# Experts of a routed MLP: sorted by token count and taken four at a time, in place of fixed pairs in rounds

## What is computed

```python
def expert_mlp(t, w1, w3, w2):
    return (jax.nn.silu(t @ w1) * (t @ w3)) @ w2

def hier_moe(h, w_rg, b_rg, w_re, b_re, w1, w3, w2):
    ...                     # best of 4 groups, then the best 2 of its 8 experts, per token
    cw = jnp.einsum('tk,tkn->tn', wts, jax.nn.one_hot(eid, N_EXPERTS, dtype=F32))
    y = jnp.zeros_like(t)
    for e in range(N_EXPERTS):
        y = y + (cw[:, e:e + 1] * expert_mlp(t, w1[e], w3[e], w2[e])).astype(t.dtype)
    return y.reshape(shp)
```

## Time and profile before

| | |
|---|---|
| Median of three runs | 1081.12 us |
| Lowest of the three | 1079.55 us |
| Profiled execution, its own time | 1078.98 us |
| Its span, first to last instruction | 1077.5 us |
| Mean granted TensorE clock | 0.985 of 2.4 GHz |
| TensorE busy with products | 1024.2 us (95%) |
| VectorE, ScalarE busy | 332.3 us, 365.1 us |
| Moved by DMA | 284.14 MB, 127505 packets |

### The profile page before, as it was taken

One profiled execution on the slowest core, in us unless ns is written; L12 is line 12 of the kernel. 1 busy time (PEld: TensorE's weight loads), 2 busy tenths in 40 slices (PEclk: granted clock), 3 DMA queues, 4 the chain that ended last, 5 costly groups with the idle time before them and its releaser, 6 DMA issues.

```text
span 1077.5 us, 14121 instructions
## 1 busy us (share of the span) xinstructions
PE 1024.2 (95%) x5184; PEld 615.0 (57%) x5184; DVE 332.3 (31%) x803; ACT 365.1 (34%) x659; POOL 65.8 (6%) x110
## 2 busy tenths in 40 slices
PE   4799999999999999999998999999999999999994
PEld 2568686868687877788765444444334444444441
DVE  2345555555545454552223111010110111110013
ACT  6263637373737373720023212222112221222212
POOL 1020202020202020200000000000000000000000
PEclk9899999999999999999997999999999999999997
DMA  9946262627272715237873999999999999999920
GB/s 347 312 111 180 84 186 77 193 70 200 63 205 58 212 51 156 78 117 230 350 305 130 378 418 417 429 422 422 421 418 420 420 420 419 421 430 422 420 98 40
DMA packets 127505, 284.14 MB, mean 264 GB/s; under 512 B 6336, under 2 KB 100736, under 8 KB 115200
## 3 DMA queue, kind: packets, MB, share of 16 engines
q1 hardware_dynamic: 127152, 283.82, 70.7%
q10 hardware_dynamic: 336, 0.10, 0.0%
HBM read 282.86 MB, written 1.05 MB: 263 GB/s over the span
## 4 chain that ended last, share of the span: by engine, by line
PE 89%; DVE 3%; issue 3%; DMA 2%; SPq 1%; ACT 1%; POOL 0%; DVEq 0%; ACTq 0%; POOLq 0%
PE bank L480 35%; PE bank L775 21%; PE bank L783 10%; PE bank L767 6%; PE bank L793 6%; PE bank L710 3%; DMA arena<-in_w_mod 2%; DVE arena L1487 2%; PE bank L505 1%; PE bank L814 1%; SPq L302 1%; PE bank L512 1%; PE bank L584 1%; PE bank L601 1%; PE bank L610 1%
## 5 line engine op out<-in xcount | busy, mean ns | idle before, releaser
L480 PE MATMUL bank<-arena 128*128 128x256 f32 (+3 forms) x1792 | 403.1, 382 | 4.4 <-DVE arena L1156 3.8
L480 PEld LDWEIGHTS bank<-arena 128*128 128x128 f32 x1792 | 298.9, 191 | 95.1 <-issue 65.6
L775 PE MATMUL bank<-arena 128*64 128x512 f32 x1024 | 226.0, 594 | 0.9 <-ACT arena L1039 0.9
L775 PEld LDWEIGHTS bank<-arena 128*64 128x64 f32 x1024 | 72.1, 137 | 149.9 <-issue 149.9
L783 PE MATMUL bank<-arena 128*64 128x512 f32 x512 | 113.4, 595 | 0.0
L1487 DVE TENSOR_TENSOR arena<-arena,bank 128x512 f32<-128x512 f32 x16 | 16.5, 1029 | 253.3 <-PE bank L775 253.3
L1052 ACT ACT_TABLE_LOAD x16 | 20.5, 1283 | 194.1 <-PE bank L775 194.1
L1491 DVE COPY arena<-bank 128x512 f32<-128x512 f32 x32 | 22.1, 691 | 170.5 <-PE bank L783 170.5
L783 PEld LDWEIGHTS bank<-arena 128*64 128x64 f32 x512 | 35.3, 137 | 65.9 <-issue 64.0
L767 PE MATMUL bank<-arena 128*128 128x128 f32 x544 | 65.8, 281 | 0.6 <-DVE arena L1452 0.6
L767 PEld LDWEIGHTS bank<-arena 128*128 128x128 f32 x544 | 64.2, 197 | 0.7 <-DVE arena L1452 0.7
(11 more groups left out here) (275 smaller groups left out, 879.4 us busy)
## 6 DMA issues: line engine op xcount, KB each, us to landing
arena<-in_w SPq DMA_DIRECT2D x96, 2048.0 KB, 12.1
arena<-in_w_in SPq DMA_DIRECT2D x72, 512.0 KB, 7.0
arena<-in_w_mod SPq DMA_DIRECT2D x12, 2048.0 KB, 8.1
arena<-in_w_proj_a SPq DMA_DIRECT2D x8, 512.0 KB, 3.8
arena<-in_w_proj_b SPq DMA_DIRECT2D x8, 512.0 KB, 5.3
arena<-in_w_out SPq DMA_DIRECT2D x2, 2048.0 KB, 9.8
arena<-in_x SPq DMA_DIRECT2D x4, 512.0 KB, 5.4
arena<-in_ctx SPq DMA_DIRECT2D x2, 512.0 KB, 6.7
```

Of the source, the lines that this page charges most:

```text
L480: i = mm(dst, w(k), rhs(k), start=k == 0, stop=k == KT - 1)
L775: i = mm(acc[SLOTS * b:SLOTS * b + SLOTS, :], xg[:, k, SLOTS * b:SLOTS * b + SLOTS], wtile(kind, b, j)[:, k, :], start=k == 0, stop=k == K ...
```

## The change

The rounds and the fixed pairs are replaced by a list. Experts 0 to 3 stay first, as two pairs with 64 slots each, while VectorE sorts the other 28 by their counts. The 24 with fewer tokens follow as six units of four, with `NARROW` = 32 slots each; the four fullest (`TOP`) come last, in pairs with 64 slots, in a loop of `n_pairs` turns that begins with them and goes on with extra items. An extra item is a further visit to an expert that has more tokens than the slots it was given, and it loads that expert's matrices again. With no such expert `n_pairs` is 2. The eight units before the loop are written out, so `UNROLL` and the loop over groups of pairs go.

What is used more than once: columns of `rk` and `ck` are ranks and weights in list order, `ids_i` the expert numbers, which SyncE reads into registers one by one (`chosen`); `LOADS` is the list of the 84 loads before the loop, `PLACE` their slots. The accumulating banks are no longer cleared by a product with zeros (`zb`); the first `combine`, in unit 1, starts them. The constants, slots and semaphore values:

```diff
-PAIRS = NE // 2
+NARROW = 32
+FIXED = 4
+TOP = 4
+
+UNITS = [(e, 2) for e in range(0, FIXED, 2)] + [(c0, 4) for c0 in range(FIXED, NE - TOP, 4)]
+NU = len(UNITS)
+C_ITEM = NE - TOP
+N_EXTRA = 16
+COLS = NE + N_EXTRA + 2
...
+        KINDS = ("w1", "w3", "w2")
+        LOADS = [(u, k, b) for u, (_, n) in enumerate(UNITS) for k in KINDS for b in range(n)]
+        PLACE = {load: i % len(RING) for i, load in enumerate(LOADS)}
+
+        def wslot(kind, b, u):
+
+            if u == NU:
+                return ring[(len(LOADS) + 2 * KINDS.index(kind) + b) % len(RING)]
+            return ring[PLACE[u, kind, b]]
+
+        def wtile(kind, b, u):
+
+            return wslot(kind, b, u).rearrange("p (k n) -> p k n", n=D if kind == "w2" else F)
+
+        def arrived(u):
+
+            return 16 * sum(UNITS[v][1] for v in range(u % 2, u + 1, 2))
```

SyncE's loads:

```diff
-            for j in range(UNROLL):
-                load_pair(j, j, (2 * j, 2 * j + 1))
-            sp.wait_ge(S("rounds_ready"), 1)
-            n_rounds = sp.value_load(rcnt_i[0:1, 0:1], min_val=1, max_val=T // SLOTS)
-            with sp.Fori(1, n_rounds * (PAIRS // UNROLL)) as g:
-                for j in range(UNROLL):
-                    e = [sp.snap((g & (PAIRS // UNROLL - 1)) * (2 * UNROLL) + (2 * j + b)) for b in range(2)]
-                    load_pair(g * UNROLL + j, j, e)
+            def free(u, kind):
+
+                if kind == "w2":
+                    sp.wait_ge(S("my"), this(u, 1))
+                else:
+                    sp.wait_ge(S({"w1": "m1", "w3": "m3"}[kind]), this(u))
+
+            def chosen(column):
+
+                return sp.value_load(ids_i[0:1, column], min_val=0, max_val=NE - 1)
+
+            for n, (at_u, k, b) in enumerate(LOADS):
+                c0, wide = UNITS[at_u]
+                if n == 5:
+                    sp.wait_ge(S("proj_mm1"), KT // 2)
+                if n == 7:
+                    sp.wait_ge(S("rt_mm"), 1)
+                    sp.wait_ge(S("ssq_out"), 8)
+                if k == "w1" and b == 0:
+                    if c0 == FIXED:
+                        sp.wait_ge(S("ids_ready"), 1)
+                    experts = [c0 + i if c0 < FIXED else chosen(slice(c0 + i, c0 + i + 1)) for i in range(wide)]
+                if n >= len(RING):
+                    free(*LOADS[n - len(RING)][:2])
+                sp.dma_start(wslot(k, b, at_u), src[k][experts[b]]).then_inc(S(f"in_{k}_{at_u % 2}"), 16)
+
+            sp.wait_ge(S("items_ready"), 1)
+            n_pairs = sp.value_load(n_i[0:1, 0:1], min_val=TOP // 2, max_val=(TOP + N_EXTRA) // 2)
+            with sp.Fori(0, n_pairs) as p:
+                experts = [chosen(bass.ds(p * 2 + (C_ITEM + b), 1)) for b in range(2)]
+                for k in KINDS:
+                    free(p + (NU - 1), "w2" if k == "w2" else "w3")
+                    for b in range(2):
+                        sp.dma_start(wslot(k, b, NU), src[k][experts[b]]).then_inc(S(f"in_{k}_0"), 16)
```

TensorE's products (`down` changes as `up` does, with the halves of w2):

```diff
-            def up(acc, kind, j):
-
+            def up(acc, kind, u, n):
+
+                w = P // n
                 for k in range(KT):
-                    for b in range(2):
-                        i = mm(acc[SLOTS * b:SLOTS * b + SLOTS, :], xg[:, k, SLOTS * b:SLOTS * b + SLOTS],
-                               wtile(kind, b, j)[:, k, :], start=k == 0, stop=k == KT - 1)
+                    for b in range(n):
+                        i = mm(acc[w * b:w * b + w, :], xg[:, k, w * b:w * b + w],
+                               wtile(kind, b, u)[:, k, :], start=k == 0, stop=k == KT - 1)
                 return i
...
-            def pair(j, q, loads):
+            def unit(u, q, n, loaded):
 
                 pe.wait_ge(S("xgc"), this(q, 1))
-                pe.wait_ge(S(f"in_w1_{j % 2}"), loads * 32)
-                up(UX, "w1", j).then_inc(S("m1"), 1)
-
-                combine(q - 1)
-                pe.wait_ge(S(f"in_w3_{j % 2}"), loads * 32)
-                up(VY, "w3", j).then_inc(S("m3"), 1)
+                pe.wait_ge(S("in_w1_" + loaded[0]), loaded[1])
+                up(UX, "w1", u, n).then_inc(S("m1"), 1)
+
+                if u > 0:
+                    combine(q - 1, u == 1)
+                pe.wait_ge(S("in_w3_" + loaded[0]), loaded[1])
+                up(VY, "w3", u, n).then_inc(S("m3"), 1)
...
-            pe.wait_ge(S("rounds_ready"), 1)
-            n_rounds = pe.value_load(rcnt_i[0:1, 0:1], min_val=1, max_val=T // SLOTS)
-            with pe.Fori(0, n_rounds) as r:
-
-                pe.wait_ge(S("acc_read"), r + 1)
-                for t in range(2):
-                    for hf in range(2):
-                        mm(ACC[t][hf][:], zb[:, 0:P], zb[:], start=True, stop=False, skip_group_check=True)
-                with pe.Fori(0, PAIRS // UNROLL) as g:
-                    for j in range(UNROLL):
-                        pair(j, r * PAIRS + g * UNROLL + j, r * (PAIRS // 2) + g * (UNROLL // 2) + (j // 2 + 1))
-                q = r * PAIRS + PAIRS - 1
-                combine(q)
+            for at_u, (_, n) in enumerate(UNITS):
+                unit(at_u, at_u, n, (str(at_u % 2), arrived(at_u)))
+            pe.wait_ge(S("items_ready"), 1)
+            n_pairs = pe.value_load(n_i[0:1, 0:1], min_val=TOP // 2, max_val=(TOP + N_EXTRA) // 2)
+            with pe.Fori(0, n_pairs) as p:
+                unit(NU, p + NU, 2, ("0", p * 32 + (arrived(NU - 2 + NU % 2) + 32)))
+            combine(n_pairs + (NU - 1))
```

VectorE's list and its units (`one_hots`, `weighted`, `gated` and `rows_y` are what stood in the loop before, for `n` experts; the lines left out between unit 1 and unit 3 work out the extra items):

```diff
+            one_hots(0, 2, 0)
+            ts(rank, rt[:, 11], 1.0, None, ALU.subtract)
+            dve.memset(rk[:, :, COLS - 2:], -1.0)
+            dve.memset(ck[:, :, COLS - 2:], 0.0)
+            dve.memset(ids_f, 0.0)
+            cp(ck[:, :, 0:FIXED], cw[:, :, 0:FIXED])
             dve.wait_ge(S("rank_mm"), 2)
-            link(dve.tensor_reduce(rcnt[:, 0:1], bank[1][:, 0:NE], AX.X, ALU.max))
-            link(ts(rcnt[:, 1:2], rcnt[:, 0:1], float(SLOTS), 1.0, ALU.is_gt, ALU.add))
-            link(stt(rcnt[:, 2:3], rcnt[:, 0:1], float(2 * SLOTS), rcnt[:, 1:2], ALU.is_gt, ALU.add))
-            link(stt(rcnt[:, 3:4], rcnt[:, 0:1], float(3 * SLOTS), rcnt[:, 2:3], ALU.is_gt, ALU.add))
-            cp(rcnt_i[:], rcnt[:, 3:4].to_broadcast([P, 4])).then_inc(S("rounds_ready"), 1)
-            dve.wait_ge(S("rounds_ready"), 1)
-            n_rounds = dve.value_load(rcnt_i[0:1, 0:1], min_val=1, max_val=T // SLOTS)
...
-                step = Chain("res_step", r * 4)
+            link(cp(cnt, bank[1][:, 0:NE]))
+
+            ts(key[:, 0:FIXED], slot_no[:, 0:FIXED], -1.0, 64.0 * T, ALU.mult, ALU.add)
+            link(stt(key[:, FIXED:], cnt[:, FIXED:], float(NE), e_no[:, FIXED:], ALU.mult, ALU.subtract))
+            link(tt(table, along(key, NE), down_(key, NE), ALU.is_gt))
+            link(dve.tensor_reduce(pos, table, AX.X, ALU.add))
+            n_quad = NE - FIXED - TOP
+            tt(order[:, 0:n_quad, :], along(pos, n_quad), down_(slot_no[:, FIXED + TOP:NE], NE), ALU.is_equal)
+            link(tt(order[:, n_quad:, :], along(pos, TOP), down_(slot_no[:, FIXED:FIXED + TOP], NE), ALU.is_equal))
+            link(sums(ids_f[:, FIXED:NE], order, e_no))
+            cp(ids_i[:, 0:NE], ids_f[:, 0:NE]).then_inc(S("ids_ready"), 1)
+
+            weighted(0, 2, 0)
+            dve.wait_ge(S("hw"), this(0))
+            one_hots(2, 2, 1)
+            for src_, dst in ((rank, rk), (cw[:], ck)):
                 for t in range(2):
-                    dve.wait_ge(S("mc"), this(r * (PAIRS + 1) + PAIRS, t))
-                    for hf in range(2):
-                        s = slice(512 * hf, 512 * hf + 512)
-                        i = tt(res[:, s], ACC[t][hf][:], gate2[:, s], ALU.mult)
-                    step(i)
-                    step(tt(x1[:, t, :], x1[:, t, :], res, ALU.add))
-                dve.memset(ct, 0.0)
-
-                ts(rank, rank, float(SLOTS), None, ALU.subtract).then_inc(S("acc_read"), 1)
-                dve.wait_ge(S("acc_read"), r + 2)
+                    link(sums(dst[:, t, FIXED:NE], order, src_[:, t, :]))
+            gated(0)
+            rows_y(0)
...
+            weighted(FIXED, 4, 2)
+            dve.wait_ge(S("hw"), this(2))
+            one_hots(FIXED + 4, 4, 3)
+            link(sums(ids_f[:, NE:NE + N_EXTRA], picked, e_no))
...
+            for q in range(3, NU):
+                c0, n = UNITS[q]
+                weighted(c0, n, q)
+                dve.wait_ge(S("hw"), this(q))
+                one_hots(c0 + n, 4 if q + 1 < NU else 2, q + 1)
+                gated(q)
+                rows_y(q)
+            dve.wait_ge(S("items_ready"), 1)
+            n_pairs = dve.value_load(n_i[0:1, 0:1], min_val=TOP // 2, max_val=(TOP + N_EXTRA) // 2)
+            with dve.Fori(0, n_pairs) as p:
+                q = p + NU
+                weighted(p * 2 + C_ITEM, 2, q)
+                dve.wait_ge(S("hw"), this(q))
+                one_hots(p * 2 + (C_ITEM + 2), 2, q + 1)
+                gated(q)
+                rows_y(q)
```

(24 more changed lines are left out.)

192 lines of the change are left out of this document (102 added, 90 removed).

## The result

Four runs of each kernel in turn on one chip: 1056.05 us after (1055.67 to 1057.06) against 1080.53 us before, a ratio of 0.978 (95%: 0.976 to 0.980). The change takes 24 us off, 2.2%. One of the four runs of the kernel before took 3790.51 us; it counts in the median given, but not in the ratio. The forecast was 1052.6 us, 3.4 us lower. The profiled execution took 1057.06 us, its span is 1055.2, 5.4 more than the sum gave.

The account below looks back on a forecast made before the run. TensorE bounds the kernel at 29.9 us a unit, transfers 0.6 us behind. Span 1077.5 - 28.5 - 0.7 + 1.0 + 0.5 = 1049.8 us, plus 1.5 around it and 1.3 for the median: 1052.6; range 1047 to 1060, with three rivals 1046 to 1065.

Parts of the forecast that it names:

- the sum: Whole kernel: 1077.5 - 28.5 - 0.7 + 1.0 + 0.5 = 1049.8 us of span.
- The bound: Expert stage: TensorE sets the pace at 29.9 us a pair; transfers, at 29.3, stand 0.6 us behind as next bound.
- The quad's cost: Units of four: 64 records take 7.1 us, so a quad costs TensorE 29.9 us, against 58.5 us of transfers.
- the rival that they don't: Quads: four column groups don't overlap, 0.44 us a record, +211 us, 1264 us; chance 0.03.
- The clock: Quads: TensorE's clock falls in waits of 5 to 10 us; each stage loses about 2.3 us, hidden behind transfers.
- The list and the new waits: VectorE's sorting list and SyncE's register loads ahead of load 12: taken as nothing, at worst 3 us.
- term of 1.0 us for TensorE's register load: Between unit 7 and the loop: the load costs 0 to 3.7 us, taken as 1.0.
- The rate: Weight stream from load 8 on: 430 GB/s, 4.88 us a load, with bounds of 426 to 434 (-4 to +4 us).
- The rival of 420: Expert stage: transfers give no more than 420 GB/s, the dip being part of their work; +9 us, 1061; chance 0.12.
- 0.8 to its receipt: Unit 8's w1, load 85: bytes in at 969.2 us, landing counted 0.8 us later, at 970.0.
- the sum's bubble: Load 18 waits for unit 1's w2 product, a gap in the stream of about 0.5 us.
- Nothing ahead of it changes: Unit 0's w1 product: ends at 586.86 us in both kernels, so load 8 goes then.

Follow-up runs that it names:

- before with a thin `combine`: Kernel before, 16 pairs, with `combine` adding 32 of 512 output columns, the rest left out: 1056.12 us, ratio 0.978 (two runs).
- filler: Unused TensorE products in the changed kernel's router waits: 1053.48 us; with the fullest experts' pairs before the quads 1054.21, and with more products in the last quad 1050.76.
- kernel without the loop: Changed kernel with the fullest experts' pairs right behind the fixed pairs, quads last, no loop or extra items: 1055.27 us, ratio 0.976.

## Why the forecast was right, and by what it was off

The span is 5.4 us above the sum, and the three largest errors have the same sign. The time is off by 3.4 only, by luck: I had added 1.3 us because two of the three runs of before stood above the profiled one, and the profiled run after stands 1.0 above its median.

**The bound.** Right. Before, TensorE set the pace: 1/6 fewer bytes of w3 changed nothing. After, the transfers do: such a cut gives 36 us. The next bound stood right behind the first, as the sum had it; before with a thin `combine` meets the same floor without a single quad.

**The quad's cost.** I took 7.1 us for 64 records out of 6.9 to 7.7; it is 7.07 at 2.4 GHz. Four column groups overlap in full, and the rival that they don't has fallen.

**The clock.** As forecast, it falls in the quads' waits (0.79 on average from 660 to 975 us), and a product behind a wait takes 8.4 to 9.8 us for 7.07, so it loses 1.3 to 2.7 us, around the 2.3 taken, hidden in waits of 5 to 11 us. By the Trainium skill's "TensorE: Matmul & The Clock Gate", section HAM oscillation, each burst behind a DMA wait starts cold; the trace agrees for the 16 products behind waits of 4.8 to 11.3 us, while the one behind 3.06 us took 7.07. In the quads nothing of it shows: before with a thin `combine` makes the same stretch at a clock of 0.99 in 454.8 us, against 455.4. In the router nothing hides it: there the traces without filler have a clock of 0.58 to 0.67, and the way to the first w1 product is 1.5 and 2 us shorter in two of the three traces with filler, and no shorter in the third.

**The list and the new waits.** Nothing, as taken. The term of 1.0 us for TensorE's register load before the loop was not seen (-1.0).

**The rate.** The prediction took 430 GB/s; over 315 us it is 428, 4.90 us a load: 78 x 0.023 = +1.8 us. The rival of 420 has fallen: the dip to 320 was the ring run dry, and the stream doesn't have it. The prediction set the Trainium skill's 358 GB/s for a core against the trace. The same page, "DMA: Bandwidth & Descriptors", section Measured, calls that the share of a core when both of a pair stream, and has 425 for one alone, in a load of 16 MB: with 428 for one core, the trace agrees.

**The step that was off most for its size** is "0.8 to its receipt". I worked it out from a lone load. With w1 of unit 8 due at 970.0, plus the 1.8 of the rate and 1.7 of the late start, it should have begun at 973.5, and by the sum's bubble 974.0. It began at 976.32, behind a wait for DMA, so +2.3. The bytes tell how this divides. By the view of DMA the queue that carries the weights (q1) had moved 163.6 MB, 78 loads, from load 8 to 973.7 us, 0.5 later than the sum with these corrections has it; and the last of the 78 counts as landed 2.6 us behind its bytes, 1.8 more than I took. In four more traces of this order it is 2.4 to 3.9 us. Whether that is because the load's parts run on sixteen engines that are not equally far, or the receipts queue, no run here tells. It is less where nothing follows: in the three traces with the quads last, the last load of all landed 1.1 to 1.7 us behind its bytes. The cause stays open. The Trainium skill, "DMA: Bandwidth & Descriptors", section Latency and other measured facts, has HBM's latency at 0.2 us on average and 2 us at high load, with a receipt that makes up most of a transfer's fixed cost; 0.8 for a lone load and 2.6 in the stream go that way, but that they are the same delay no run here shows.

**The start.** "Nothing ahead of it changes" was right of the program and wrong of the time: the first w1 product came at 581.54 and not 579.84, +1.7 us. TensorE's order of time after, at head 0 of the mixer:

```profile
41.41 3.85 PE L517 MATMUL bank<-arena 128*128 128x262 f32 x8 [3.88 <-DVE arena L1194]
```

The earlier trace rows has this product at 39.42. In the traces of both kernels and all experiments it starts anywhere from 39.3 to 42.5 us, with no order by kernel (39.42 and 42.48 with the code of before, 41.41, 42.33 and 39.98 with that of the change). In this trace the last modulation products took 3.33 us. A single profile carries some 3 us of that, and I compared sums over one with each other.

**The end.** Units 8 to 9: 30.6 us for 29.9, +0.7, in which TensorE waits 0.45 us for DMA; the window from 975 to 1000 shows 384 GB/s. The loads of the last two units use fixed slots and go round six of the eight, and one wait serves both turns: w1 of unit 9 is loaded once unit 8's w3 product is done (994.0 us), though it goes where unit 8's w1 stood, which was free at 983.4. Between 990 and 998 us the transfers run at 197 to 385 GB/s. The forecast had them at 428 to 432 up to 1015 us. The kernel without the loop has the same wait and the same dip. From the end of the last w2 product to the end of the span are 18.3 us for 19.2, 0.25 more gained than taken. The last bytes of the experts moved at about 1025 us, and not 1019 as I had it.

The terms: 1.7 + 1.8 + 2.3 + 0.7 - 1.0 - 0.25 = 5.25 of the 5.4 us of span.

**Where the rest of the gain stayed.** Sixteen units of 29.9 us became ten, so some 180 us of TensorE's work went. 28.5 of it was forecast to turn into time and 1058.28 - 1036.93 = 21.4 did at that place; 126 us are waits for DMA, and 16 products behind such waits at 8.4 to 9.8 us for 7.07 take some 32.

**Where the gain came from.** Not for the most part from faster transfers. Loads 84 and 85, counted from 0, are used before by this product, and after by the one at 976.32:

```profile
998.40 7.04 PE L775 MATMUL bank<-arena 128*64 128x512 f32 x32
```

Their bytes were in at 980.4 us before and at 973.7 after, 6.7 us sooner. The other 15.4 of the 22.1 us come from the ring: before, the two matrices lay in it for 18.0 us until TensorE came to them, and after for 2.6. At the other end it shows too: the last bytes moved at 1029.9 us before and at 1025.4 after, 4.5 us sooner, while the last w2 product ended 21.4 sooner.

## What to carry to other kernels

Where one resource bounds a loop and the next stands 2% behind it, a cut in the first is worth the 2% and what it does to the ends of the loop, however large it is. The ends can be the larger part: here some 15 of 22 us were full slots that waited for TensorE. Halve the transfers in a copy of either kernel to see on which side it stands. A stage that waits for the last of n loads and frees n slots at its end needs a ring for both; count it before widening the stage. And once transfers set the pace, look for the places that they don't hide: the last unit behind the last byte, and stretches like the router here, where TensorE's clock was at 0.58 to 0.67. One profile can't tell terms of under 3 us from what differs between two executions.
